# Scratch additions on GpSimd in the first output projection, and thirty more products after the last one

## The reference, cut to what matters

```
h = x + retention_layer(x)          # w_in 2048 x 12288, then w_out 4096 x 2048
h = h + pooling_layer(h)            # w_in 2048 x 8192, w_grp 4 x 1024 x 1024, w_out 4096 x 2048
x = rms_norm(h)
x = x + rmsnorm((gate_a * y_a + gate_b * y_b) @ w_out)
x = x + rmsnorm(sigmoid(x @ w_ple_gate) * (p @ w_ple_proj))
```

## Time and profile before

| | us |
|---|---|
| median of 3 runs | 2627.43 |
| lowest and highest | 2626.55, 2628.14 |
| profiled execution, span from first to last instruction | 2625.2 |
| the median less that span | 2.2 |
| PE busy | 2608.3 (99% of the span) |
| VectorE busy | 1960.7 (75%) |
| ScalarE busy | 1321.5 (50%) |
| GpSimd busy | 162.3 (6%) |

### The profile page before, as it was taken

One profiled execution on the slowest core, in us unless ns is written; L12 is line 12 of the kernel. 1 busy time (PEld: TensorE's weight loads), 2 busy tenths in 40 slices (PEclk: granted clock), 3 DMA queues, 4 the chain that ended last, 5 costly groups with the idle time before them and its releaser, 6 DMA issues.

```text
span 2625.2 us, 36689 instructions
## 1 busy us (share of the span) xinstructions
PE 2608.3 (99%) x13284; PEld 2218.5 (85%) x13284; DVE 1960.7 (75%) x2764; ACT 1321.5 (50%) x1683; POOL 162.3 (6%) x329
## 2 busy tenths in 40 slices
PE   9999999999999999999999999999999999999998
PEld 7888888888888888888889999998888888788887
DVE  5887877776755766757457786977798999989565
ACT  5444444444444444444446455454666666564453
POOL 0000000000000000000000331413000000000000
PEclk9999999999999999999999999999999999999999
DMA  8555555555655555556555555645565655655754
GB/s 301 181 187 176 183 185 185 185 192 185 199 196 190 192 198 188 197 190 212 196 189 178 173 164 162 195 155 179 176 196 190 198 192 185 201 189 193 247 175 159
DMA packets 152395, 499.70 MB, mean 190 GB/s; under 512 B 28816, under 2 KB 29552, under 8 KB 151728
## 3 DMA queue, kind: packets, MB, share of 16 engines
q1 hardware_dynamic: 149456, 486.18, 56.2%
q0 software_dynamic: 2784, 11.40, 1.4%
HBM read 493.30 MB, written 4.21 MB: 190 GB/s over the span
## 4 chain that ended last, share of the span: by engine, by line
PE 97%; DVE 2%; ACT 1%; issue 0%; DMA 0%; SPq 0%; POOL 0%; DVEq 0%; ACTq 0%
PE PS L1925 27%; PE PS L1926 27%; PE PS L1927 27%; PE PS L1950 4%; PE PS L1952 4%; PE PS L1953 4%; PE PS L2091 2%; DVE yl L1619 1%; DVE wlo L1074 1%; PE PS L2098 0%; PE PS L1961 0%; PE PS L2107 0%; DMA raw<-in_stream 0%; DVE yl L1610 0%; PE PS L2005 0%
## 5 line engine op out<-in xcount | busy, mean ns | idle before, releaser
L1074 DVE TENSOR_TENSOR wlo<-raw,whi 128x1024 fp32r<-128x1024 f32 x899 | 1097.6, 1225 | 598.0 <-ACT whi L622 593.2
L622 ACT CAST whi<-raw 128x1024 fp32r<-128x1024 f32 x899 | 939.7, 1049 | 1180.3 <-PE PS L1927 1004.5
L1925 PE MATMUL PS<-whi,aH 128*128 128x512 f32 x2160 | 844.2, 391 | 4.4 <-DVE wlo L1074 3.3
L1926 PE MATMUL PS<-wlo,aH 128*128 128x512 f32 x2160 | 840.6, 389 | 0.0
L1927 PE MATMUL PS<-whi,aL 128*128 128x512 f32 x2160 | 840.6, 389 | 0.0
L1925 PEld LDWEIGHTS PS<-whi,aH 128*128 128x128 f32 x2160 | 405.5, 188 | 89.6 <-issue 3.3
L1927 PEld LDWEIGHTS PS<-whi,aL 128*128 128x128 f32 x2160 | 405.4, 188 | 84.6
L1926 PEld LDWEIGHTS PS<-wlo,aH 128*128 128x128 f32 x2160 | 405.6, 188 | 83.0
L1950 PE MATMUL PS<-aH,whi 128*128 128x256 f32 x768 | 220.8, 288 | 1.5 <-DVE aL L1110 1.5
L1952 PE MATMUL PS<-aL,whi 128*128 128x256 f32 x768 | 217.1, 283 | 0.0
L1953 PE MATMUL PS<-aH,wlo 128*128 128x256 f32 x768 | 217.1, 283 | 0.0
(11 more groups left out here) (357 smaller groups left out, 2564.6 us busy)
## 6 DMA issues: line engine op xcount, KB each, us to landing
raw<-in_stream SPq DMA_DIRECT2D x899, 512.0 KB, 3.3
xT<-in_xT SPq DMA_DIRECT2D x8, 256.0 KB, 6.2
H<-in_x SPq DMA_DIRECT2D x4, 512.0 KB, 8.7
pB<-in_pool_b POOLq DMA_DIRECT2D x4, 512.0 KB, 4.4
iT<-diag_in SPq DMA_DIRECT2D x16, 128.0 KB, 3.1
bg<-in_b_gate POOLq DMA_DIRECT2D x8, 256.0 KB, 3.6
out<-eb SPq DMA_DIRECT2D x8, 256.0 KB, 2.3
dmask<-in_dmask SPq DMA_DIRECT2D x4, 384.0 KB, 5.3
```

What stands on the lines that cost most here:

```text
L622: nc.scalar.copy(whi[:, s], raw[:, s]).then_inc(hi_done, 1 + blank)
L1074: nc.vector.tensor_tensor(wlo[:, s], raw[:, s], whi[:, s].bitcast(F32), ALU.subtract).then_inc(lo_done, 1 + blank)
L1925: mm(out, hi[:, kt + k, tok], whi[:, s, k], start=kt + k == 0, stop=False)
L1926: mm(out, hi[:, kt + k, tok], wlo[:, s, k], start=False, stop=False)
```

## The change

GpSimd gets, between its last retention head and the load at L517, two memsets and twelve additions. They wait until quarter 0 of the first output projection is in `H` (`h_out` at 3). `mz` and `pB` are tiles of the pooling layer, 1024 elements per partition each, not yet in use; both are written again before they are read. Each addition reads `mz` and `pB` and writes `pB`, and waits for the one before.

```diff
@@ GpSimd, behind the loop over the retention heads
+            pool.wait_ge(h_out, 2 + 1)
+            nc.gpsimd.memset(mz[:], 0.5).then_inc(rrs_done, 1)
+            nc.gpsimd.memset(pB[:], 0.5).then_inc(rrs_done, 1)
+            for n in range(12):
+                pool.wait_ge(rrs_done, 2 * R_N + n + 2)
+                nc.gpsimd.tensor_tensor(pB[:], mz[:].rearrange("p t n -> p (t n)"), pB[:], ALU.add).then_inc(rrs_done, 1)
+            pool.wait_ge(rrs_done, 2 * R_N + 14)
+
```

```diff
@@ TensorE, behind the last product
+            def spare(stationary, moving, rows=P, width=NB):
+                mm(PS[0:rows, 6, 0:width], stationary, moving, start=True, stop=True, skip_group_check=True)
+
+            for n in range(3):
+                spare(aH[:, n, 0:P], whi[:, 0, 0])
+            for n in range(3):
+                spare(aH[:, 0, 0:P], whi[:, 0, n % 2])
+            for n in range(3):
+                spare(aH[:, n, 32:P + 32], whi[:, 0, 0])
+            for n in range(3):
+                spare(aH[:, n, 96:P + 96], whi[:, 0, 0])
+            for n in range(3):
+                spare(aH[:, n, 0:P], whi[:, 0, 0, 32:], width=480)
+            for n in range(3):
+                spare(aH[:, n, 0:P], whi[:, 0, 0, 96:], width=416)
+            for n in range(3):
+                spare(aH[:, n, 96:P + 96], whi[:, 0, 0, 96:], width=416)
+            for n in range(3):
+                spare(aH[:, n, 16:P + 16], whi[:, 0, 0])
+            for n in range(3):
+                spare(aH[:, n, 0:P], whi[:, 0, 0, 0:416], width=416)
+            for n in range(3):
+                spare(aH[:, n, 0:96], whi[:, 0, 0], 96)
```

## The result

The kernel with both edits takes 2641.73 us (median of 4 runs, 2640.85 to 2642.78), the kernel before on the same chip 2627.78 (4 runs, 2626.55 to 2629.12). The ratio is 1.0054 with a 95% interval of 1.0041 to 1.0066: slower by 13.95 us, where 9.8 was forecast.

The account below looks back on a forecast made before the run. TensorE was taken as the bound from start to end. A stall of 8.3 us plus 1.5 for the clock, products free, gave 9.8 on 2627.4: 2637.2 us; range 2628 to 2643.

Parts of the forecast that it names:

- Place and direction: First output projection, quarter 1: TensorE waits for `wlo` before chunk 12, 7 to 9 us (computed 8.3); slower, chance 0.77.
- The start: GpSimd's first addition, after `h_out` and two memsets of 0.94 us each, starts at about 610.0.
- Taking turns: First output projection: GpSimd additions and VectorE operations with two SBUF inputs alternate, needing P + 0.94 per subtraction, P + 0.15 per piece.
- P: Time of one GpSimd addition of 1024 elements, taken as 2.15 us, bounds 1.75 to 2.7.
- Rival A: At the four pieces and subtraction 8, VectorE keeps its turn and TensorE never waits: 2627.4 us, chance 0.20.
- The length of one addition: GpSimd, 1024 elements: 2.15 us, extended from small additions at 1.92 ns per element.
- Until subtraction 7 the lag is within the slack: Quarter 1: subtraction 7 ends at 634.9 against 634.3, so only the four pieces afterwards break the slack.
- The clock: Behind the gap before chunk 12, TensorE's clock falls to 1.2 GHz; the return costs 1.5 us, bounds 0 to 3.
- The range: Whole kernel: the forecast's own range 2631 to 2643 us, widened to 2628 by Rival A's upper edge.
- Hidden products: Tail: thirty TensorE products take 6.4 us, end 2.7 us before the span's end and cost nothing.
- Rival B: Tail: the products run past the end, 2629.9 us alone or 2639.7 with the stall; chance 0.05.
- What is late next: nothing: After subtraction 8, subtractions 9 to 11 follow at 1.14 us each, faster than 2.72, so nothing else is late.

Follow-up runs that it names:

- the copies: Kernel with the change, its twelve GpSimd additions replaced by twelve copies of 1024 elements (one tensor read), no products behind the last one; executed once, span 2625.1 us.
- adds_eight: Kernel before plus the GpSimd edit with eight additions instead of twelve, without the thirty products: 2630.28 us, ratio 1.0010 to the kernel before.
- clock_held: Kernel before plus the twelve additions, no thirty products, and 32 extra TensorE products on bank 7 before chunk 12 of quarter 1: 2641.94 us median.

## Why the prediction was right, and where its sizes were off

**Place and direction** held. The forecast was one wait for `wlo` of 7 to 9 us before chunk 12; it was 8.1. That this number fits so well is luck: it was computed as the whole stall (8.3), which was 11.1, and the gap is 8.1 only because the chunks ahead of it had already slipped by 2.8. It was to be paid in full, since TensorE is the bound; 13.73 us of the quarter became 13.95 of the medians.

**The start** of the additions was computed as 610.0 and was 611.54. The run had reached this stage 1.6 us late; against the addition into `H` both are 3.2 to 3.3.

**Taking turns** held. Additions and subtractions alternated while both were waiting, also in the pieces (10.07 us for four). The 3.34 us from subtraction to subtraction are P + 0.94 with P = 2.40. A piece and an addition took 2.5 us, P + 0.1 where P + 0.15 was computed. One addition alone, eight turns of 3.34 and three of 2.5 make 36.6 for the twelve, and they took 36.59. Rival A, VectorE keeping its turn, fell at once with the first three subtractions. The other point from which A was to decide, P under 1.47, was met by the copies with 1.04, and their time is that of before. The sentence of the Trainium skill that the prediction took up at this rival (whoever issues first has the shared ports for the whole instruction) stands on its page (SBUF — State Buffer, "Who interferes with whom") for VectorE's two-port modes, not for GpSimd's instructions. For the additions of 1024 elements it came out so here: no subtraction or piece ended before the addition that it had met.

**The length of one addition** is the first term of the wrong size: taken as 2.15, measured 2.40. The slope of 1.92 ns per element, from additions of 24 to 76 elements, had to be stretched thirteenfold; up to 1024 elements it is (2.40 - 0.333) / 948 = 2.18. With 2.40 the prediction's own sum puts the end of subtraction 8 at 619.4 + 12 x 2.40 + 1.6 (the late start) = 649.8, and it was 649.5. The stall by it is 649.8 + 0.1 - 638.6 = 11.3; it was 2.84 + 8.27 = 11.1. The Trainium skill (GPSIMD Engine Reference, section 3.1) would have given 2.25 as an estimate, half of its figure for 2048 elements: nearer, but low as well.

**"Until subtraction 7 the lag is within the slack"** failed, and not by the size of P alone: the prediction's own 634.9 is already 0.6 us past the 634.3 at which TensorE wants chunk 11. With P = 2.40 it becomes 617.66 + 8 x 2.40 = 636.9, 2.6 us past. That is the row of small waits, and adds_eight shows it by itself, 2.9 us. It isn't a cost besides the stall: what TensorE loses there it doesn't lose in the gap.

**The clock** is the second term. It fell as the earlier trace rows said it would, but the return was taken as 1.5 us and cost 2.1 by the quarter of clock_held, 2.6 by the rows of after; both lie in the bounds of 0 to 3. Since 2.15 instead of 2.40 is 3.0 us and 1.5 instead of 2.1 to 2.6 is about 1, the two explain nearly all of the 4.15 us between 9.8 and 13.95.

**The range** doesn't follow from its own terms. P from 1.75 to 2.7 and the clock from 0 to 3 give 2627.4 + 3.5 = 2630.9 to 2627.4 + 14.9 + 3 = 2645.3, not 2643. The measured 2641.73 lies inside both, but only 1.3 us below the stated end.

**Hidden products** held: 6.4 us predicted, 6.68 measured, the last one ends 2.5 us before the span does, ratio alone 0.9997. Rival B is out: the products stand (6.68 - 0.39) / 29 = 0.217 us apart where the sum by columns has 6.4 / 30 = 0.213, so the offsets cost next to nothing, and the products reach the end only when doubled.

**What is late next: nothing** held too. Subtractions 8 to 11 followed in 4.62 us, and no chunk behind them shows a wait.

## What to carry to other kernels

Work on GpSimd that reads SBUF isn't free beside a VectorE that has two SBUF inputs: count both queues in turn, here P + 0.94 us for a subtraction of 1024 elements and P + 0.1 for a piece of 256, and compare that with what the bound engine gives for a turn. Several short VectorE instructions between two that the bound engine waits for are the costly place, since each of them takes a whole turn; look for them before anything else. And judge a repair by the whole kernel and not by its stage: here 2.1 us won in one stage came back, in the executions that were profiled, as waits for small loads a thousand microseconds later.

## What the runs showed of the hardware that I had not expected

- A single read tensor on GpSimd is enough to alternate with VectorE (1.75 to 2.06 us for a subtraction of 1.23), while 30 us of pure writing cost it nothing.
- Whether the clock falls isn't told by the wait's length alone: it stayed at 1.00 through a wait of 2.7 us in the projection, fell to 0.54 and 0.50 in waits of 4.3 and 8.1 there, and fell to 0.75 and 0.67 in the delta stage around waits of no more than 1.3. At the start of the run TensorE waits 1.98 us before 13.02 in the profile of after and 1.97 before 12.97 in that of before; from 12 to 16 the granted clock is 0.66 in the one and 1.00 in the other.
- 64 empty instructions of TensorE cost no time that could be told (ratio 1.0000, 0.9991 to 1.0009) and left the fetch at the second group where it was (1593.6 and 1593.7); with 32 real products (clock_held) it came 0.5 us behind the last load's issue and not 4.8 to 5.9. Whether such a fetch is what makes one of the loads take 3.0 to 4.0 us, and TensorE wait, stays open.
